# Eight gated-head projections in three f32r passes in the input stage, none left in the delta stage

## The reference, cut to what matters

```python
for l in range(DEPTH):                      # DEPTH = 2
    h = rms_norm(x, pre_mix_g[l])
    a_q, a_f, a_i, a_g, b_q, ..., d_q, d_k, d_v, d_beta, d_a, d_z = split_columns(h @ w_in[l])
    o_a = hgrn2_mixer(a_q, a_f, a_i, a_g, ...)   # "gated heads": sigmoids of a_q, a_f, a_g
    ...
    o_d = gdn_mixer(d_q, d_k, d_v, d_beta, d_a, d_z, ...)   # gated delta rule
```

## Time and profile before

| | |
|---|---|
| median of 3 runs | 2355.86 us (2354.54 to 2357.97) |
| the profiled execution | 2351.73 us |
| its span, first to last instruction | 2349.9 us |
| mean granted TensorE clock | 0.978 |
| PE busy, share of the span | 94% |
| DVE, ACT busy | 51%, 39% |
| delta stages, from PE's first record to PE's first of the next stage | 86.88 to 208.71 us and 888.25 to 1008.80 us |

### The profile page before, as it was taken

How to read it: one execution, slowest core, us unless ns; L and a number is a source line. 1 busy time by engine, 2 the same in 40 slices (tenths; PEclk the granted TensorE clock), 3 DMA queues, 4 the chain that set the end, 5 groups by cost and what they waited for, 6 DMA issues and landing times. The chain is left out here.

```text
span 2349.9 us, 35192 instructions
## 1 busy us (share of the span) xinstructions
PE 2212.0 (94%) x14460; PEld 1541.0 (66%) x14460; DVE 1190.6 (51%) x2045; ACT 906.2 (39%) x1611; POOL 46.1 (2%) x36
## 2 busy tenths in 40 slices
PE   6999999899999999999998999999999988999998
PEld 4664444488888776544446888886776556886556
DVE  4633444566662285333446666524537764444444
ACT  4423235433333353223344333334346553424452
POOL 2000001000000020000010000000000000000000
PEclk8999999999999999999999999999999989999899
DMA  4101111122222220111112222212321102222000
GB/s 176 54 21 55 55 37 46 62 90 90 102 87 99 90 72 20 38 55 55 40 47 73 94 90 90 107 72 94 110 72 55 37 19 90 90 90 90 19 1 36
DMA packets 23919, 159.78 MB, mean 68 GB/s; under 512 B 3024, under 2 KB 3664, under 8 KB 4944
## 3 DMA queue, kind: packets, MB, share of 16 engines
q1 hardware_dynamic: 23760, 157.53, 18.8%
HBM read 155.43 MB, written 2.10 MB: 67 GB/s over the span
## 5 line engine op out<-in xcount | busy, mean ns | idle before, releaser
L652 DVE TENSOR_TENSOR arena_r<-ring,arena_r 128x512 fp32r<-128x512 f32 x428 | 297.6, 702 | 475.4 <-ACT arena_r L643 471.0
L643 ACT ACTIVATE arena_r<-ring 128x512 fp32r<-128x512 f32 x428 | 266.9, 632 | 637.1 <-PE banks L693 601.0
L691 PE MATMUL banks<-oT_r,arena_r 128*128 128x512 f32 x1024 | 424.4, 414 | 19.0 <-DVE arena_r L914 14.4
L693 PE MATMUL banks<-oT_r,arena_r 128*128 128x512 f32 x1024 | 407.5, 398 | 0.0
L692 PE MATMUL banks<-hT_r,arena_r 128*128 128x512 f32 x928 | 369.0, 398 | 0.0
L727 PE MATMUL banks<-hT,ring 128*128 128x512 f32 x544 | 262.6, 611 | 0.0
L691 PE MATMUL banks<-arena_r,arena_r 128*128 128x512 f32 x592 | 238.7, 403 | 13.4 <-DVE arena_r L683 10.8
L692 PE MATMUL banks<-arena_r,arena_r 128*128 128x512 f32 x624 | 246.1, 394 | 0.0
L691 PEld LDWEIGHTS banks<-oT_r,arena_r 128*128 128x128 f32 x1024 | 194.4, 190 | 78.4 <-DVE arena_r L914 17.0
L693 PE MATMUL banks<-arena_r,arena_r 128*128 128x512 f32 x592 | 233.0, 394 | 0.0
L693 PEld LDWEIGHTS banks<-oT_r,arena_r 128*128 128x128 f32 x1024 | 194.1, 190 | 46.6
(11 more groups left out here) (392 smaller groups left out, 2937.5 us busy)
## 6 DMA issues: line engine op xcount, KB each, us to landing
ring<-weights SPq DMA_DIRECT2D x142, 1024.0 KB, 4.7
xT<-x_features SPq DMA_DIRECT2D x2, 1024.0 KB, 6.2
arena<-memory SPq DMA_DIRECT2D x2, 1024.0 KB, 4.8
y_features<-xT SPq DMA_DIRECT2D x8, 256.0 KB, 2.0
const<-constants SPq DMA_DIRECT2D x1, 1088.0 KB, 7.7
const<-constants SPq DMA_DIRECT2D x1, 512.0 KB, 8.4
arena<-positions SPq DMA_DIRECT2D x1, 256.0 KB, 2.7
small<-small_vectors SPq DMA_DIRECT2D x2, 68.5 KB, 6.4
```

The source lines that it names most:

```text
L643: act.activation(hi, self.stream.block(b, n), ACT.Copy).then_inc(self.chip.sem("hi_ready"), 1)
L652: vec.tensor_tensor(lo[:, 0:n * P], self.stream.block(b, n), hi[:, 0:n * P].bitcast(F32), ALU.subtract).then_inc(self.chip.sem("lo_ready"), 1)
L691: pe.matmul(out, w_hi, hi, start=k == 0, stop=False)
L693: ins = pe.matmul(out, w_lo, hi, start=False, stop=k == nk - 1)
```

## The change

The eight units of the gated heads are put behind the nine of the input stage, in the order q, f, g, i, and computed by three f32r passes there. The sigmoids that ScalarE did from PSUM in the delta stage are done in the input stage on the emptied tiles. The tiles of the low input parts and of the split weights move to numbers that the new results don't use. In the delta stage, every `meanwhile` call and the stage's weight loads go; nothing is put in their place.

```diff
+HGRN_UNITS = (("q", 0), ("q", 1), ("f", 0), ("f", 1), ("g", 0), ("g", 1), ("i", 0), ("i", 1))
+HGRN_EARLY = 8
...
-    for n in "iqfg":
-        for i in range(2):
-            p.unit(f"a{n}{i}", "w_in", KD, cols(256 * "qfig".index(n) + P * i))
+    for n, i in HGRN_UNITS:
+        p.unit(f"a{n}{i}", "w_in", KD, cols(256 * "qfig".index(n) + P * i))
...
-    u0, u1 = stream.units("misc", "dz1")
+    early = HGRN_UNITS[:HGRN_EARLY]
+    first = {"q": AQ, "f": AF, "g": AG, "i": AI}
+    u0, u1 = stream.units("misc", "a%s%d" % early[-1])
...
+    gates = len(dst)
+    dst += [chip.t(first[n] + i) for n, i in early]
...
-    hi, lo = chip.o_r, lambda k: chip.t_r(DZS + 2 + k)
-    split = Split(chip, stream, u0, u1, pairs_of(chip.t_r, DZS + 2 + KD, 4), group=GROUP)
+    LO, SPLITS = 33, ((29, 30), (31, 32), (41, 42), (44, 49))
+    hi, lo = chip.o_r, lambda k: chip.t_r(LO + k)
+    split = Split(chip, stream, u0, u1, [(chip.t_r(i), chip.t_r(j)) for i, j in SPLITS], group=GROUP)
...
+                if gates <= i < len(dst) and early[i - gates][0] != "i":
+                    n, e = early[i - gates]
+                    act.wait_ge(chip.sem("dense_used"), i + 1)
+                    if n == "q":
+                        act.activation(chip.t(AQS + e), dst[i], ACT.Sigmoid)
+                    else:
+                        if n == "f":
+                            act.activation(chip.t(AK + e), dst[i], ACT.Sigmoid, scale=-1.0)
+                        act.activation(dst[i], dst[i], ACT.Sigmoid)
...
-    meanwhile = Meanwhile(chip, stream, u0, u1, evac, chip.h)
...
-            stream.loads(sp, u0, u1)
...
             for e in range(2):
                 pe.wait_ge(chip.sem("nt_ready"), e + 1)
                 product("n", e, NT, IDENT)
-                meanwhile.tensor(pe, blocks=2)
             for e in range(2):
                 pe.wait_ge(chip.sem("x16_ready"), e + 1)
                 after(f"n{e}")
                 product("n2_", e, N16T, N16)
                 product("n2t_", e, N16, N16T)
-                meanwhile.tensor(pe, blocks=1)
...
             for c in range(1, NCH - 1):
                 t, zz = c // 2, c % 2
-                meanwhile.tensor(pe, blocks=1)
```

More of the change, by code:

```diff
@@ L958, in _ @@
                     act.activation(cv[i - 1], raw[i - 1], ACT.Copy, scale=chip.s("conv_d", 4 * (i - 1) + 3)).then_inc(chip.sem("cut_ready"), 1)
-                if 7 <= i < len(dst):
+                if 7 <= i < gates:
                     act.wait_ge(chip.sem("dense_used"), i + 1)
                     act.activation(chip.t(DZS + i - 7), dst[i], ACT.Sigmoid)
+                if gates <= i < len(dst) and early[i - gates][0] != "i":
[7 more added lines that the diff above has]
+                        act.activation(dst[i], dst[i], ACT.Sigmoid)
                 if 0 <= i - 3 < 6:
@@ L1071, in delta_stage @@
     with nc.Block() as block:
-        @block.sync
-        def _(sp):
-            stream.loads(sp, u0, u1)
         @block.tensor
@@ L1133, in _ @@
             turned("v1", v_feat[1])
-            meanwhile.tensor(pe, blocks=3)
             for i in (0, 1):
                 made(pe.matmul(fill(f"norm{i}"), chip.c("blk64"), sq[i], start=True, stop=True))
-            meanwhile.tensor(pe, blocks=2)
             pe.wait_ge(chip.sem("lg_ready"), 1)
@@ L1279, in _ @@
                             ins.then_inc(chip.sem("o_ready"), 1)
-            meanwhile.tensor(pe, blocks=4)
             pe.wait_ge(chip.sem("sq_ready"), 2)
@@ L1283, in _ @@
                 made(pe.matmul(fill(f"out{h}"), chip.c("blk64"), SQ[h], start=True, stop=True))
-            meanwhile.tensor(pe)
         @block.scalar
@@ L1321, in _ @@
                 empty(f"eb{h}", EB[h], ACT.Exp, scale=-1.0)
-            meanwhile.scalar(act, 1)
             for e in range(2):
@@ L1351, in _ @@
                 rstd_of(f"out{h}", RN[h], 64.0)
-            meanwhile.scalar(act)
         @block.vector
```

## The result

The changed kernel takes **2363.32 us** (median of 7 runs, 2360.25 to 2366.85), the kernel before 2356.41 on the same chips (7 runs). The ratio is 1.0026, with a 95% interval of 1.0015 to 1.0038. Five more runs of the changed kernel beside 20 of the one before gave 1.0035 (1.0021 to 1.0049). So it is slower by some 7 us, where 51 were forecast. The forecast of 2407 and its range from 2370 on both missed; the rival "it falls only at the serial end" (2359) came closest.

A forecast was written before the change was run, and what follows sets the result against it. PE's order of work was taken to bound the delta stages. Input +88.6, seam -4.0, delta stages -(242.4 - 204), next stages' starts +5.0 gave +51 us: 2355.9 + 51 = 2407, range 2370 to 2425.

The forecast's parts named there:

- it falls only at the serial end: Rival: in the delta stage only the state loop loses the clock; stage 79 us, sum +3 us, 2359; chance 0.08.
- I take the clock to fall at about 20 us and to stay low nearly to the end: Main case, delta stage: low clock for 40.5 us of own work, adding 29.4 us net; stage 102 us; chance 0.76.
- what comes back is wide work; what doesn't bring it back is narrow work: Rule read from the earlier trace: wide products restore PE's full clock, narrow ones don't; applied to the delta stage's small products.
- rows 8: Profile rows at 1185 us: clock falls after narrow 64-row matmuls and a 1.39 us gap, staying 0.52 through 3 busy us.
- The price of the low clock: Delta stage: each us of own work at the low clock takes 0.85 us more, +34.4 before 5 us taken off.
- Own work at full clock: Delta stage: PE's work without projections, 59.4 us, less 2.5 for the slow start, gives 57.0 us.
- Waits: Delta stage: PE waits that the projections had covered, 15.3 us in sum, with 0.3 for the stage's end.
- The input stage: Eight added units at PE's pace of 5.54 us each, 44.3 us a layer, with loads and splits hidden.
- The seam: Between input and delta stage: PE's wait falls from 3.3 to 1.3 us, saving 2.0 us a layer.
- rows 8 and 9: The 1185 us rows, plus those at 2198 us: clock falls after a 3.05 us gap, stays 0.50 to 2212.
- the rival that it holds: Rival: full clock throughout both delta stages, sum -12.4 us, 2343 as a median; chance 0.12.
- the two sums of 72.7 and 102: Predicted delta stage lengths in us: 72.7 at full clock, 102 with the low clock's net 29.4 added.

The follow-up runs named there:

- experiment 4: Changed kernel with PE held some 8 us by eight unused GpSimd operations ahead of the inversion, so only 64 x 64 products follow; 2386.13 us in one run.
- experiment 5: Changed kernel with PE held some 8 us ahead of the inversion, then 20 unused products of 64 rows x 128 columns against 512; 2399.66 us in one run.
- experiment 3: Changed kernel with 16 unused 128 x 512 products a layer in the delta stage's waits; 2359.28 us, 1.0018 of the kernel before.
- experiment 1: Changed kernel with two of eight units back in the delta stage, 16 float32 blocks placed in PE's waits and behind the norm; 2333.98 us, ratio 0.9909.
- experiment 2: Changed kernel with four of eight units back in the delta stage as 32 float32 blocks, nine of them behind the norm; 2337.64 us, ratio 0.9933.
- experiment 8: Changed kernel with one unit back in the delta stage, 8 blocks in waits outside the state loop; 2352.78 us, ratio 0.9991.
- experiment 7: Kernel of experiment 1 with one block moved from ahead of w to behind the second half's d group; 2335.61 us, ratio 0.9923.

## Why the prediction was wrong

**The step that failed** is "I take the clock to fall at about 20 us and to stay low nearly to the end". It rested on "what comes back is wide work; what doesn't bring it back is narrow work". The clock is at 1.00 through the inversion, experiment 4 shows narrow products bringing it back, and experiment 5 shows it for the very shape of rows 8. The 29.4 us a layer that this step added are 4 to 5 us in the first layer. PE was busy 11.9 us at the low clock in that stage (windows from 138.9, 179.9 and 193.6 us above), of which not quite half is lost; against the 57.2 us of own work at full clock it was busy 4.3 us longer.

**The price of the low clock** was right: the x125 group takes 5.30 us against 3.88 before, and 3.20 us of it lie at the low clock. So 1.78 us of work took 3.20, 0.80 more per us; 0.85 was predicted. The mechanism was there, for 13.7 us of the stage (10.2 in the second layer) instead of most of it.

**The delta stage otherwise.** Own work at full clock: predicted 57.0, measured 57.2 (experiment 3). Waits: 18.4 us (79.91 less 61.53) against 15.3 and 0.3. The predicted ones came as forecast: 2.41 for 2.6, 1.34 for 1.3, 1.18 for 1.1, 0.63 for 0.5, 1.16 for 1.1, 0.38 and 0.39 for 0.5 a step, 1.56 for 1.5, 1.18 for 1.4, and 3.18 at the end for 2.7 and 0.3. What the sum lacked are the two issue gaps, 3.0 us. So the stage was 57.2 + 18.4 and 4.3 for the clock. (The prediction's terms add up to 56.9 where it has 57.0, and to 72.6 where it has 72.7.)

**The input stage.** 44.3 predicted; a unit takes 5.60 us in the first layer and 5.55 in the second, eight 44.8 and 44.4, and PE has no gap there, as forecast. Why the first layer's units are 0.05 longer stays open. The seam is 1.33 in both layers (1.3 predicted), where 3.30 and 3.73 stood before. The next stage is 2.0 and 1.8 us longer, of which its start costs 1.6 and 1.7 (2.5 predicted): L730's six records take 3.92 us, where L727's six took 2.74.

**The rival that won** said 79 us for the stage and +3 us. It was given 0.08, because rows 8 and 9 were taken for a rule about shapes. What they show is only that the clock falls after short waits too, and so it did here, at the corner and in the state loop, behind gaps of no more than 1.5 us in a sparse stretch. It also fell once ahead of the inversion, at 138.9 us, behind the gap of 2.41. The Trainium skill, "TensorE: Matmul & The Clock Gate", section "Why this matters for your kernels", by which only long gaps lose the clock, would have given the rival that it holds, 73 us a stage; the trace of after doesn't agree, since the clock fell twice behind gaps under 1.6 us. The Trainium skill, "TensorE: Matmul & The Clock Gate", section "A second HAM failure mode: psum-queue depth-cycling", tells of a clock that swings because PE idles briefly but often; the trace of after agrees at those two places and not in the inversion. The stage of 79.9 us lay between the two sums of 72.7 and 102, nearer to the first.

**Why there is no gain.** The blocks have another price at each place, which the delta stages show (means of both layers):

| float32 blocks in the delta stage | its length | added per block |
|---|---|---|
| 0 (changed) | 78.6 | |
| 16 (experiment 1) | 78.3 | 0.0 |
| 32 (experiment 2) | 90.1 | 0.73 |
| 64 (before) | 121.2 | 0.97 |

Two runs aren't in it: the second profile of the changed kernel has 79.8 in both layers, and experiment 8, with 8 blocks, 79.4.

A block in the input stage costs 5.60 / 8 = 0.70 us. The last 32 gained 0.27 each by the move, some 8.6 us a layer, the middle 16 next to nothing (0.5), and the first 16 lost 0.70 each, 11.2 us a layer: they had been free, since they filled waits and kept the clock up. With 2.0 saved at the seam and 1.9 lost in the next stage that makes 8.6 + 0.5 + 2.0 - 11.2 - 1.9 = -2.0 us a layer, a loss of 4 us in both, where 7 were measured. The other 3 aren't accounted for; 1 of them could be the stages of 79.8 in the second profile, and the low clock in the attention stage moves as much from profile to profile. The cheaper passes gave, and the uncovered waits took it back. Leaving the 16 in the waits gives the lowest median here, 0.9909 of the time before.

What stays open: whether the 4.8 and 5.3 us that experiment 1 leaves open can be filled too; only one other placing (experiment 7) was tried. And what decides, from run to run, whether the clock falls in a sparse stretch.

## What to carry to other kernels

Work that one engine does while another is waited for has a price by its place, not by its kind: before moving it out, count the waits that it covers, and leave there as much as they hold. When a stretch of the trace shows a slow state, read on to where it ends before you take it for a rule, since the end tells what brings the state back. A filler (here unused work) in a serial stretch can pay for itself by what it keeps (the clock, time for the next instructions to arrive), so take it out by experiment, not by sum.

## What the runs showed of the hardware

- **Narrow products keep the clock and bring it back.** After 7.8 us of waiting, 64 x 64 products in float32 had the clock at 1.00 again in 3.6 and 5.3 us (experiment 4) and kept it for 23.9 us in the first layer; products of 64 rows against 512 took 3.6 and 5.8 us (experiment 5).
- **Long runs of short products run dry.** PE had nothing to start for 1.51 and 1.47 us in the changed kernel (1.52, 1.77 and 1.79 in others) in the runs of 64 x 64 and 32 x 32 products at the stage's end. With three wide products among them, the gaps were gone or 0.39. Each of the 34 such gaps in the 11 profiles ends 1.2 to 1.6 us after a 16 KB packet of the instruction queue has ended. Wide products elsewhere don't help: in experiment 3, with 16 of them, gaps of 1.17 and 1.77 us remain.
- **Whether the clock falls in a sparse stretch differs from run to run.** The second delta stage of the changed kernel had 10.2 and 13.7 us at the low clock in its two profiles (77.3 and 79.8 us), and the attention stage of the first layer had 13.8 and 6.9 (84.0 and 80.7 us).
